# Delta rule: the 16x16 diagonal blocks inverted by forward substitution on GpSimd, three doubling levels kept of six

## The reference

```python
decay = exp(where(incl, G[i] - G[j], -inf))
A = where(strict, beta * (k @ k.T) * decay, 0)      # strictly lower, chunk x chunk
T = solve_triangular(eye + A, eye)                  # (I + A)^-1
u = T @ (beta * v);  w = T @ (beta * exp(G) * k)
```

## Time and profile before

| | us |
|---|---|
| median of 3 runs | 1391.96 (1390.5 to 1393.2) |
| the profiled execution | 1391.32 |
| its span in the trace | 1389.6 |
| TensorE busy | 1255.4 (90%) |
| VectorE busy | 766.4 (55%) |
| ScalarE busy | 597.9 (43%) |
| GpSimd busy | 90.1 (6%) |
| mean granted clock of TensorE | 0.955 |

### The profile page before, as it was taken

How to read it: one execution, slowest core, us unless ns; L and a number is a source line. 1 busy time by engine, 2 the same in 40 slices (tenths; PEclk the granted TensorE clock), 3 DMA queues, 4 the chain that set the end, 5 groups by cost and what they waited for, 6 DMA issues and landing times.

```text
span 1389.6 us, 21774 instructions
## 1 busy us (share of the span) xinstructions
PE 1255.4 (90%) x8505; PEld 1124.6 (81%) x8505; DVE 766.4 (55%) x1016; ACT 597.9 (43%) x859; POOL 90.1 (6%) x190
## 2 busy tenths in 40 slices
PE   5979999999999999999997999996199999999980
PEld 4979999999999999999997999995166666666650
DVE  5435456455453654545546454424477777777755
ACT  5423333333333333333333232225077777777752
POOL 0010000000000000000001000000401001001003
PEclk9999999999999999999998999998599999999995
DMA  5271120211212212112120233565679999999736
GB/s 195 85 201 46 63 83 32 83 53 54 83 40 67 66 45 81 47 54 75 46 68 20 72 101 128 172 270 227 249 269 352 361 350 354 356 352 352 242 106 212
DMA packets 53196, 212.34 MB, mean 153 GB/s; under 512 B 6001, under 2 KB 8577, under 8 KB 44689
## 3 DMA queue, kind: packets, MB, share of 16 engines
q1 hardware_dynamic: 39664, 176.05, 37.1%
q0 software_dynamic: 8208, 27.36, 5.8%
q10 hardware_dynamic: 5264, 8.13, 1.6%
HBM read 182.59 MB, written 28.93 MB: 152 GB/s over the span
## 4 chain that ended last, share of the span: by engine, by line
PE 82%; DVE 6%; DMA 5%; ACT 3%; issue 2%; POOL 1%; SPq 0%; POOLq 0%; ACTq 0%; DVEq 0%
PE proj L632 29%; PE proj L1354 10%; PE wideB L1382 7%; PE proj L998 5%; PE small L1361 4%; PE wideB L399 4%; PE wideA L406 3%; PE proj L941 3%; PE wideA L1336 2%; PE proj L1368 2%; PE wideB L413 2%; DMA wraw<-in_w_in 2%; PE small L998 2%; PE small L362 1%; POOL scr_rows L1837 1%
## 5 line engine op out<-in xcount | busy, mean ns | idle before, releaser
L632 PE MATMUL proj<-xnh,whi 128*128 128x288 f32 x1152 | 350.6, 304 | 13.3 <-DVE ubuf L740 7.1
L632 PE MATMUL proj<-xnl,whi 128*128 128x288 f32 x1152 | 350.7, 304 | 0.0
L632 PE MATMUL proj<-xnh,wlo 128*128 128x288 f32 x1152 | 350.6, 304 | 0.0
L632 PEld LDWEIGHTS proj<-xnh,whi 128*128 128x128 f32 x1152 | 220.9, 192 | 14.4 <-DVE ubuf L740 7.3
L632 PEld LDWEIGHTS proj<-xnl,whi 128*128 128x128 f32 x1152 | 220.6, 192 | 0.0
L632 PEld LDWEIGHTS proj<-xnh,wlo 128*128 128x128 f32 x1152 | 220.6, 191 | 0.0
L1457 DVE TENSOR_TENSOR gu_lo<-gu_raw,ehi 128x2048 fp32r<-128x2048 f32 x66 | 148.0, 2284 | 0.0
L644 DVE TENSOR_TENSOR wlo<-wraw,whi 128x1024 fp32r<-128x1024 f32 x72 | 88.0, 1223 | 71.5 <-ACT whi L640 71.5
L1448 ACT ACTIVATE ehi<-gu_raw 128x2048 fp32r<-128x2048 f32 x66 | 125.6, 1905 | 0.0
L640 ACT ACTIVATE whi<-wraw 128x1024 fp32r<-128x1024 f32 x72 | 75.9, 1055 | 75.5 <-PE proj L632 59.5
L1354 PE MATMUL proj<-ehi,xs 128*128 128x512 f32 x264 | 97.6, 473 | 1.5 <-DVE xs L1476 1.5
(11 more groups left out here) (317 smaller groups left out, 2344.8 us busy)
## 6 DMA issues: line engine op xcount, KB each, us to landing
wraw<-in_w_in SPq DMA_DIRECT2D x72, 512.0 KB, 3.4
gu_raw<-in_w_gate SPq DMA_DIRECT2D x33, 1024.0 KB, 9.1
gu_raw<-in_w_up SPq DMA_DIRECT2D x33, 1024.0 KB, 11.8
dn_raw<-in_w_down SPq DMA_DIRECT2D x33, 1024.0 KB, 5.8
wraw<-in_w_out SPq DMA_DIRECT2D x24, 512.0 KB, 4.0
xb<-scr_rows POOLq DMA_DIRECT2D x33, 256.0 KB, 9.0
scr_y<-yout POOLq DMA_DIRECT2D x33, 256.0 KB, 7.3
scr_gate<-gate ACTq DMA_DIRECT2D x16, 288.0 KB, 2.1
```

Source lines behind the costliest of these rows:

```text
L632: mm = pe.matmul(out, w[:, kc, :], x[:, kc, hh * HALF:(hh + 1) * HALF], start=(j == 0), stop=(j == 23))
```

## The change

Levels 0 to 2 are gone. In their place the eight 16x16 diagonal blocks of each of the five units are inverted by forward substitution on GpSimd. Every partition holds one column of one block's inverse, for all five units (`column`, 128x5x16), and the block itself (`lanes`, 128x16x5x16). To bring a block to the 16 partitions of its columns, SP writes the eight diagonal blocks to DRAM (8 DMAs, each 16 partitions by 5 pieces of 64 bytes), waits for all of them, and loads them back with each block repeated for 16 partitions (one DMA of 128 x 5120 bytes, 640 KB). GpSimd sets `column` to unit columns and then does 15 pairs of a multiplication and a subtraction over 5 x (15-k) elements for k = 0 to 14, each waiting for the one before it. VectorE spreads the columns over `TT` with one masked product at slot 24, and TensorE turns it at slot 25. Levels 3 to 5 stand at slots 27 to 34, the scan at 35 to 46, the output's norm at 47 to 49, its turning at 52 and its write to `yb` at 53. The projection's and the fill's slots stay.

```diff
+LANE, BASE = 16, 3
+STEPS = LEVELS - BASE
+LANE_STEPS = 2 * LANE - 1
...
+    scr_lanes = nc.dram_tensor("scr_lanes", (P // LANE, LANE, UNITS, LANE), F32, kind="Internal").ap()
...
-        NORMS_AT, V_AT, SPREAD_AT, GRAMS_AT, TURN_AT0 = 1, 2, 4, 7, 9
-        LEVEL_STEPS = [(k, step) for k in range(LEVELS) for step in range(3 if k < LEVELS - 1 else 2)]
-        LEVEL_AT = {11 + n: at_level for n, at_level in enumerate(LEVEL_STEPS)}
-        scan0 = 29
+        NORMS_AT, V_AT, SPREAD_AT, GRAMS_AT, EXPAND_AT, TURN_AT0 = 1, 2, 4, 7, 24, 25
+        LEVEL_STEPS = [(k, step) for k in range(BASE, LEVELS) for step in range(3 if k < LEVELS - 1 else 2)]
+        LEVEL_AT = {27 + n: at_level for n, at_level in enumerate(LEVEL_STEPS)}
+        scan0 = 35
...
-            if p == 46:
+            if p == 52:
                 pe.wait_ge(s["o_scaled"], n)
...
                 dve.tensor_tensor(AT[:, :], wideB[:, 0:UW], buf2[:, 0:UW], ALU.mult).then_inc(s["a_cut"], 1)
-                dve.tensor_tensor(attnT[:, :], wideA[:, 0:UW], buf2[:, 0:UW], ALU.mult).then_inc(s["attn_set"], 1)
                 dve.wait_ge(s["a_cut"], n)
                 dve.wait_ge(s["c_set"], 2 * n)
                 dve.tensor_tensor(units(AT[:, :]), units(AT[:, :]), spread(sts(ST_C)), ALU.mult)\
                    .then_inc(s["a_set"], 1)
-                dve.wait_ge(s["a_set"], n)
-                dve.tensor_tensor(units(TT[:, :]), units(AT[:, :]), level_mask(0), ALU.mult).then_inc(s["tt_cut"], 1)
-                dve.wait_ge(s["tt_cut"], n)
-                dve.tensor_tensor(units(TT[:, :]), units(TT[:, :]),
-                                  ident.unsqueeze(1).to_broadcast([P, UNITS, P]), ALU.add).then_inc(s["tt_set0"], 1)
+                dve.tensor_tensor(attnT[:, :], wideA[:, 0:UW], buf2[:, 0:UW], ALU.mult).then_inc(s["attn_set"], 1)
+            if p == EXPAND_AT:
+                dve.wait_ge(s["lane_step"], LANE_STEPS * n)
+                blocks = [P, UNITS, P // LANE, LANE]
+                dve.tensor_tensor(TT[:, :].rearrange("p (u b i) -> p u b i", u=UNITS, i=LANE),
+                                  column[:, :, :].unsqueeze(2).to_broadcast(blocks),
+                                  misc[:, M_BLOCK:M_BLOCK + P // LANE].unsqueeze(1).unsqueeze(3).to_broadcast(blocks),
+                                  ALU.mult).then_inc(s["tt_set0"], 1)
...
+        def lanes_sync(sp, g):
+
+            n = g + 1
+            sp.wait_ge(s["a_set"], n)
+            for b in range(P // LANE):
+                rows = slice(b * LANE, (b + 1) * LANE)
+                sp.dma_start(scr_lanes[b], units(AT[rows, :])[:, :, rows]).then_inc(s["lanes_out"], 16)
+            sp.wait_ge(s["lanes_out"], LANE_OUT * n)
+            sp.dma_start(lanes[:, :, :, :].rearrange("p k u i -> p (k u i)"),
+                         scr_lanes.rearrange("b k u i -> b (k u i)").unsqueeze(1)
+                         .to_broadcast([P // LANE, LANE, LANE * UNITS * LANE])).then_inc(s["lanes_in"], 16)
+
+        def lanes_pool(pool, g):
+
+            n = g + 1
+            first = LANE_STEPS * g
+            wait(pool, s["tt_set0"], g)
+            pool.tensor_tensor(column[:, :, :], misc[:, M_UNIT:M_UNIT + LANE].unsqueeze(1).to_broadcast([P, UNITS, LANE]),
+                               ones[:, 0:UNITS * LANE].rearrange("p (u i) -> p u i", u=UNITS), ALU.mult)\
+                .then_inc(s["lane_step"], 1)
+            pool.wait_ge(s["lanes_in"], 16 * n)
+            for k in range(LANE - 1):
+                later = slice(k + 1, LANE)
+                pool.wait_ge(s["lane_step"], first + 2 * k + 1)
+                pool.tensor_tensor(ltmp[:, :, later], lanes[:, k, :, later],
+                                   column[:, :, k:k + 1].to_broadcast([P, UNITS, LANE - 1 - k]), ALU.mult)\
+                    .then_inc(s["lane_step"], 1)
+                pool.wait_ge(s["lane_step"], first + 2 * k + 2)
+                pool.tensor_tensor(column[:, :, later], column[:, :, later], ltmp[:, :, later], ALU.subtract)\
+                    .then_inc(s["lane_step"], 1)
...
+            LANES_BEFORE = 7
...
             with sp.Fori(1, HEADS) as i:
                 for t in range(TILES):
+                    if t == LANES_BEFORE:
+                        lanes_sync(sp, i - 1)
                     tile_load(i, t)
...
-            with sp.Fori(1, KC // 2) as j:
+            for q in (2, 3):
+                out_load(q, q % 2)
+                gate_load(q, 0, q % 2, gate)
+                if q == 2:
+                    lanes_sync(sp, HEADS - 1)
+            with sp.Fori(2, KC // 2) as j:
...
                 proj_pool(pool, i)
                 gdn_pool(pool, i - 1)
+                lanes_pool(pool, i - 1)
                 tails_pool(pool, i, 0)
                 tails_pool(pool, i, 1)
```

More of the change, by code:

```diff
@@ L175, in encoder_layer @@
         AT = sb(gd, "AT", [P, UW])
+        lanes = sb(gd, "lanes", [P, LANE, UNITS, LANE])
+        column = sb(gd, "column", [P, UNITS, LANE])
+        ltmp = sb(gd, "ltmp", [P, UNITS, LANE])
         vnorm = sb(gd, "vnorm", [P, UW])
@@ L319, in encoder_layer @@
             qk_square k_root decay t_set0 tt_set vn_set o_inter o_square o_root
-            qk_sum k_recip c_set krest_set v_scaled dgap a_cut a_set attn_set tt_cut tt_set0 x_set t_set
+            qk_sum k_recip c_set krest_set v_scaled dgap a_cut a_set attn_set tt_set0 x_set t_set
             vbar_set s_set o_set o_sum o_bias o_recip o_scaled yb_set
-            qk_copied s_zero s_in s_out""".split()
+            qk_copied lane_step lanes_out lanes_in s_zero s_in s_out""".split()
         s = {n: sem(n) for n in names}
@@ L390, in gdn_tensor @@
                 k, step = LEVEL_AT[p]
-                done = g * LEVELS + k
+                done = g * STEPS + k - BASE
                 held = level_units(k)
                 if step == 0:
-                    if k == 0:
+                    if k == BASE:
                         pe.wait_ge(s["t_set0"], n)
@@ L453, in gdn_scalar @@
                 wait(act, s["o_sum"], g)
-                wait(act, s["tat_done"], LEVELS * g)
+                wait(act, s["tat_done"], STEPS * g)
                 act.activation(buf2[:, :], sil[:, 0:2, :].rearrange("p a m -> p (a m)"), ACT.Square)\
@@ L493, in gdn_scalar @@
                        .then_inc(s["s_out"], 16)
-            if p == 43:
+            if p == 48:
                 act.wait_ge(s["o_bias"], n)
@@ L578, in gdn_vector @@
                    .then_inc(s["o_bias"], 1)
-            if p == 44:
+            if p == 49:
                 dve.wait_ge(s["o_root"], n)
@@ L584, in gdn_vector @@
                    .then_inc(s["o_scaled"], 1)
-            if p == 47:
+            if p == 53:
                 dve.wait_ge(s["o_turned"], n)
@@ L1812, in _ @@
             gdn_pool(pool, 0)
+            lanes_pool(pool, 0)
             tails_pool(pool, 1, 0)
@@ L1820, in _ @@
             gdn_pool(pool, HEADS - 1)
+            lanes_pool(pool, HEADS - 1)
             pool.wait_ge(tail_kept, 2 * HEADS)
@@ L2007, in constants @@
     parts = [i == j, i <= j, np.where(i <= j, 0.0, -1000.0), np.ones((P, P)), i < j]
-    for k in range(LEVELS + 1):
+    for k in range(BASE + 1, LEVELS + 1):
         b = 2 ** k
         cut = (i // (2 * b) == j // (2 * b)) & ((i // b) % 2 == 1) & ((j // b) % 2 == 0)
-        parts.append(-cut.astype(np.float32).T if k == 0 else -cut.astype(np.float32))
+        parts.append(-cut.astype(np.float32))
     parts.append(i % BR == np.arange(BR)[None, :])
@@ L2041 @@
     iota = spread(np.arange(40, dtype=np.float32))
+    lane = np.arange(P)[:, None]
+    unit = (lane % LANE == np.arange(LANE)[None, :]).astype(np.float32)
+    block = (lane // LANE == np.arange(P // LANE)[None, :]).astype(np.float32)
     consts = np.concatenate([table, valid, spread(a_log[0]), spread(dt_bias[0]),
-                             spread(b_router_group[0]), spread(b_router_expert[0]), iota], axis=1)
+                             spread(b_router_group[0]), spread(b_router_expert[0]), iota, unit, block], axis=1)
     w_in = np.asarray(w_in)[0]
```

19 lines of the change are left out of this document (10 added, 9 removed).

## The result

The changed kernel takes 1410.91 us in the median (1409.03 to 1421.44, 4 runs), the kernel before beside it 1391.56 (1390.5 to 1393.2, 4 runs): 1.0143 times the time, interval 1.0103 to 1.0182. It is slower by 19.3 us, where I had forecast 21 us less. The time lies in the stated range, on the other side of zero. The profiled execution took 1409.63 us, with a span of 1407.9. Some executions take about 12 us longer than others of the same kernel; in the traces that have it (experiments 1, 5, 6, 7, 8 and 10) the extra time lies behind the start of the output projection (L1040's first matmul, L998 in the kernel before), 568.0 to 570.2 us in place of 556.4 to 557.9, so beside the times I give the moment of that start.

A forecast was written before the change was run, and what follows sets the result against it. TensorE, busy 90%, was taken as the bound. A head: 79.0 + 6.5 + 2.0 + 0.5 = 88.0 against 90.97 us; seven heads -20.8, the last -3.4, its tail +3.1, together -21.1: 1371 us, range 1338 to 1424.

The forecast's parts named there:

- the clock: Fall of TensorE's granted clock behind the new wait at slot 25: 2.0 us per head.
- break-even: With G the end of slot 7's products: no gain at a 9.1 us wait; each chain microsecond costs 8 us in all.
- Removed work: On TensorE per head: three levels, 8.9 us, and the wait at slot 9, 2.0 us, go, leaving 79.0 us.
- VectorE's cut and scaling: Chain's first step: VectorE cuts AT from G + 0.29 and scales it, 2 x 0.82 us, done at G + 2.0.
- SyncE's issues: Eight stores of the diagonal blocks issued 0.47 us from start to start, the last at G + 5.3.
- The load back: Load of 640 KB from DRAM into lanes: 5.0 us, upper end 7.8, landed at G + 12.5.
- The right mechanism: Rival: load back runs on fewer queues and is late, 6.2 us, giving 1380 us; chance 8%.
- GpSimd's steps: Thirty dependent steps after the load: 10 us, plus 2.2 us contention with VectorE, ending at G + 24.7.
- steps at double price: Rival: GpSimd's thirty steps are the bound at 16.7 us, wait 13.2, time 1425 us, kernel slower; chance 32%.
- The wait: TensorE's new wait at slot 25 for VectorE's spreading product: 6.5 us per head, from 25.6 - 19.1.
- These cost nothing: Work queued behind the wait on TensorE, VectorE and ScalarE, and weights' loads behind SP's waits, add no time.
- The end of a head: Norm, turning and write at slots 47 to 53: 0.5 us per head; last head's tail +3.1 us.

The follow-up runs named there:

- experiment 1: The changed kernel without the eight stores and the load back, GpSimd's steps working on a zero lanes tile: 1328.74 us, 0.9507 times the kernel before.
- experiment 5: The changed kernel with the load back reading sixteen outermost rows of gate weights, each eight times: 1407.4 us, 1.0081 times the kernel before.
- experiment 6: The changed kernel with the load back reading 128 different outermost rows of gate weights, each once: one time, 1392.52 us.
- experiment 7: The changed kernel with the load back cut into four chunks, a semaphore each, so GpSimd starts after the first: 1381.3 us, 0.9923 times the kernel before.
- experiment 8: The changed kernel with the load in four chunks and the eight stores issued half from SyncE, half from GpSimd: 1368.86 us, 0.9803 times the kernel before.
- experiment 10: The 8x8 version with its sixteen stores on three queues and the last head's output weights loaded ahead of the lanes: 1379.61 us, 0.9909 times the kernel before.
- experiment 4: The changed kernel with the load back reading eight outermost rows of gate weights, sixteen different rows under each: one time, 1409.67 us.
- experiment 2: The changed kernel with the output weights' third tile issued ahead of the last head's stores and load of lanes: 1409.56 us, 1.0115 times the kernel before.
- experiment 3: The kernel before, six levels kept, with scan, norm, turning and write at the changed kernel's later slots: 1395.27 us, 1.0027 times the kernel before.
- 8x8 version: The changed kernel with 8x8 blocks, one level more, sixteen stores from two queues, a 160 KB load, turning at slot 22: 1371.79 us, 0.9869 times the kernel before.

## Why the prediction was wrong

The plan of the sum was right: what TensorE saves, then a chain that ends in one wait per head, then the clock. The side came out wrong because a chain with 2.6 us to spare (G + 25.6 against a break-even of G + 28.2) was 3.4 us longer. By the prediction's own rule 0.8 us beyond the break-even would cost 6.4 us in eight heads; the rest of the 19 us lies mostly in the clock and in the last head.

- **Removed work: right.** Three levels and the wait at slot 9 are gone. Undisturbed, a head is what I took: 79.0 + a wait of 9.7 + 2.2 for the clock behind it + 1.1 for another fall (below) = 92.0, and 92.3 is measured. Experiment 1 shows the saving uncovered: its heads take 80.0 us where the clock doesn't fall, with 0.8 us of waiting in them.
- **VectorE's cut and scaling: right**, G + 2.0.
- **SyncE's issues: 0.47 taken, 0.64 measured.** 1.2 us over eight. I took the spacing from two plain loads at the start; these stores have 64-byte pieces in three dimensions. Their landing, 2.2 taken, is 1.8.
- **The load back: this step failed.** I took 5.0 us with an upper end of 7.8, and it is 8.3 in this head and 8.5 to 8.7 in the six others before the last, longer than the end. The row that looked most like it, the broadcasting transfer, I used for its bytes alone. The right mechanism was among the rivals, at 8% and at 6.2 us: I doubled only the part of 3.9 us that scales with bytes. In experiments 4 to 6 the time goes by the count of outermost rows (9.16, 5.97, 3.93 us). With a load of 5.0 and the rest as measured the chain would end at G + 25.7, more if the convolution holds more steps, and by the prediction's rule the change would win. The gain would have been about half of the 21 us: with a load of 3.93 (experiment 6) the chain ends at G + 25.9, since more steps are held, and the output projection starts 11.3 us earlier than before. Experiments 6 to 8 bear out the direction: their output projections start 10 to 27 us earlier than the kernel before's.
- **GpSimd's steps: right in the sum, 12.2 taken with contention, 11.4 measured.** Behind the first two they stand 0.34 us apart, 0.33 predicted. The rival that held most of the slower side, steps at double price by themselves, is wrong: an undisturbed step costs 0.20 to 0.35 us. The contention is real, but since the load came late only two steps met it; that the sum came out is in part luck. It comes back whenever the load is made faster, up to 17.1 us in experiment 1, which is the double price after all, by another cause.
- **The wait: 6.5 predicted, 9.7 measured; the clock: 2.0 against 2.2 and 1.1.** The second term is a fall in the stretch with the norms, at a mean clock of 0.79 over 8 us, in four of six heads; the windows of one with it and one without:

```profile
380.50:388.50 8.00, 8.00 (x54) 7.98 (x54) 2.66 (x8) 0.67 (x3) 2.58 (x4) 0.79 0.23 74
...
658.00:666.00 8.00, 8.00 (x67) 8.00 (x67) 3.34 (x12) 0.51 (x2) 2.31 (x4) 1.00 0.23 74
```

  TensorE is busy throughout both; by 8 x 0.21 it costs about 1.7 us where it occurs. It isn't the new wait's doing. The kernel before has it too, in the head at 284.60:

```profile
284.60:292.60 8.00, 8.00 (x54) 7.99 (x54) 1.89 (x7) 0.51 (x2) 0.00 (x0) 0.79 0.21 66
```

  Of its four falls in six heads, two (288 and 562 us) lie in the norms and two (394 and 667) behind slot 9. The prediction took all four as what "may follow" the wait at slot 9 and removed 1.07 us per head with it. The wait went, and 1.1 us stayed. Experiment 1, with waits of 0.9 us at most, has the fall in three heads of six (350, 511 and 593 us). What sets it off stays open.
- **"These cost nothing" failed in the last head.** There the output weights' tile behind SyncE's waits is late by 9.6 us. The last head then waits 12.3 us in all, in place of 6.5. Experiment 2 shows that repairing the order alone gives nothing, since the chain holds the head for 14.4 us anyway; its load takes 1.3 us more than in the others (9.57).
- **The end of a head**: nothing per head in place of 0.5, and a tail of some 6 us in place of 3.1 (experiment 3). These nearly cancel.
- **The sum by the traces.** From the first head's norms (L369, L362 before) to the last's it takes 649.4 us against 640.4, 9.0 more; the first norms stand 1.3 us later; from the last norms to the output projection it takes 96.3 us against 89.6, 6.7 more. So the output projection starts 17.0 us later; its first group takes 11.34 us, 1.5 more than in the earlier trace rows. That makes 18.5 us, and the two spans differ by 18.3.

Slower stood at 32%, but that chance hung on the wrong term. The range rested on bounds for each term, and the load's bound was the weights' time doubled, a bound by size and not by the shape of the pattern.

## What to carry to other kernels

Price a load from DRAM to SBUF by the outermost dimension of its pattern before its bytes: here one of 640 KB took 3.9, 6.0 or 9.2 us with 128, 16 or 8 rows there. Where such a load feeds a serial consumer, split it so that the consumer starts on the first part, and share the issuing of small stores among idle queues; these two turned 1.4% slower into 2% faster. When work is moved off TensorE, work out where its chain ends before the engine would stand still, and price the wait with the clock behind it: here some 2.2 us per head, and most of it came back only when the wait was nearly gone.

## What the runs showed of the hardware that I had not expected

- One load of 640 KB in 5120-byte pieces, medians over eight heads: 8 outermost rows 9.3 us (8.6 with each piece read sixteen times), 16 rows 6.0, 128 rows 4.1. Reading the same row again was not dearer than reading others.
- SyncE's issue of that load alone took 0.62 to 0.66 us with 8 outermost rows, 0.56 with 16 and 0.34 with 128.
- An issue on SyncE's queue took 0.59 us for a store of 5 KB in 64-byte pieces, and about 0.33 us for the weights' tiles. On GpSimd's queue the issues of the 8x8 version's stores stood 0.57 us apart.
- A dependent two-input step on GpSimd over 5 to 75 elements per partition takes 0.20 to 0.35 us with 0.08 us between two; beside VectorE's two-input work most took 0.7 to 1.3 us, and thirty of them 17.1 us in place of 11.4 (experiment 1).
- TensorE's granted clock fell in a stretch in which it was busy throughout, in the kernel before as in the changed one (0.79 over 8 us).
